# Attention of a hybrid diffusion step: exponentials scaled by the inverse denominators ahead of the transposes

## The reference

```python
def softmax_with_sink(s, sink):
    sk = sink.astype(jnp.float32).reshape(N_KV_HEADS, Q_PER_KV, 1, 1)
    m = jnp.maximum(jnp.max(s, axis=-1, keepdims=True), sk)
    e = jnp.exp(s - m)
    return e / (jnp.sum(e, axis=-1, keepdims=True) + jnp.exp(sk - m))
...
    p = softmax_with_sink(jnp.concatenate([s_lat, s_ctx], axis=-1), sink)
    o = (jnp.einsum('bnkgqs,bnskd->bnqkgd', p[..., :3 * BLOCK], vband)
         + jnp.einsum('bnkgqc,bckd->bnqkgd', p[..., 3 * BLOCK:], v_ctx.astype(jnp.float32)))
```

## Time and profile before

| what | us |
|---|---|
| median of three runs | 1802.57 (1801.4, 1802.57, 1913.08) |
| the profiled execution | 1803.81 |
| its span | 1802.0 |
| TensorE busy | 1722.3 (96%) |
| VectorE busy | 1034.3 (57%) |
| ScalarE busy | 808.0 (45%) |
| GpSimd busy | 386.9 (21%) |

### The profile page before, as it was taken

The page is one execution under the profiler, slowest core; times in us unless marked ns, Lnnn a source line. Parts: engine busy times, 40 slices in busy tenths (PEclk is TensorE's granted clock), DMA queues, the critical chain, the costliest instruction groups (busy, mean ns, idle before and its releaser), DMA issues.

```text
span 1802.0 us, 45799 instructions
## 1 busy us (share of the span) xinstructions
PE 1722.3 (96%) x19547; PEld 1621.0 (90%) x19547; DVE 1034.3 (57%) x2257; ACT 808.0 (45%) x1715; POOL 386.9 (21%) x318
## 2 busy tenths in 40 slices
PE   7999998899999999999999999898999999999997
PEld 5999776779899999999989987677799999999997
DVE  5445666663583673738453556675629648365663
ACT  4433655552453452525453356464335425344352
POOL 2344010223303002020434521002260110201113
PEclk9999999999999999999999999999999999999999
DMA  9755301004613223241346270010031231323211
GB/s 329 227 141 161 99 5 49 7 15 146 172 43 99 71 71 94 68 109 53 100 141 176 71 211 5 18 34 7 26 104 32 73 98 59 106 62 92 85 57 59
DMA packets 215972, 161.09 MB, mean 89 GB/s; under 512 B 21968, under 2 KB 213146, under 8 KB 215770
## 3 DMA queue, kind: packets, MB, share of 16 engines
q1 hardware_dynamic: 213818, 156.13, 29.7%
q0 software_dynamic: 1952, 2.03, 0.4%
HBM read 154.99 MB, written 3.15 MB: 88 GB/s over the span
## 4 chain that ended last, share of the span: by engine, by line
PE 85%; DVE 6%; ACT 4%; issue 3%; SPq 1%; DMA 1%; POOL 0%; ACTq 0%; DVEq 0%; POOLq 0%
PE PS L1143 27%; PE PS L1106 19%; PE PS L1107 19%; PE PS L1066 2%; PE PS L1400 2%; PE PS L1362 2%; PE PS L1385 1%; PE PS L1000 1%; DVE mix L2631 1%; DMA mix<-in_w_in 1%; ACT mix L2017 1%; SPq L776 1%; PE PS L1599 1%; PE PS L1643 1%; PE PS L984 1%
## 5 line engine op out<-in xcount | busy, mean ns | idle before, releaser
L2784 DVE SCALAR_TENSOR_TENSOR x<-PS,mod,x 128x320 f32<-128x320 f32 (+2 forms) x240 | 90.8, 434 | 283.8 <-PE PS L1107 283.8
L836 POOL TENSOR_TENSOR SfR<-ring,SfR 128x768 fp32r<-128x768 f32 (+1 forms) x24 | 41.1, 1714 | 627.6 <-ACT SfR L1862 627.6
L1143 PE MATMUL PS<-T_hi,wsplit 128*128 128x320 f32 x768 | 170.0, 309 | 0.0
L1106 PE MATMUL PS<-in_hi,win 128*128 128x320 f32 x480 | 150.0, 320 | 0.0
L1107 PE MATMUL PS<-in_hi,win 128*128 128x320 f32 x480 | 144.6, 309 | 0.0
L1106 PE MATMUL PS<-hid_hi,wsplit 128*128 128x320 f32 x440 | 132.9, 310 | 0.0
L1107 PE MATMUL PS<-hid_hi,wsplit 128*128 128x320 f32 x440 | 132.5, 309 | 0.0
L1143 PEld LDWEIGHTS PS<-T_hi,wsplit 128*128 128x128 f32 x768 | 128.4, 188 | 0.0
L1143 PE MATMUL PS<-h_hi,wsplit 128*128 128x320 f32 x576 | 127.6, 309 | 0.0
L1143 PE MATMUL PS<-T_lo,wsplit 128*128 128x320 f32 x384 | 118.7, 309 | 0.0
L2183 ACT ACTIVATE wsplit<-Sf 128x512 fp32r<-128x512 f32 x96 | 59.8, 628 | 127.8 <-DVE Sf L2834 70.1
(11 more groups left out here) (555 smaller groups left out, 5375.5 us busy)
## 6 DMA issues: line engine op xcount, KB each, us to landing
ring<-in_w_ada SPq DMA_DIRECT2D x47, 1024.0 KB, 7.6
ring<-in_ffn_w_in SPq DMA_DIRECT2D x88, 512.0 KB, 5.2
ring<-in_ffn_w_out SPq DMA_DIRECT2D x16, 768.0 KB, 4.4
ring<-in_ffn_w_out SPq DMA_DIRECT2D x16, 640.0 KB, 4.1
ring<-in_w_in SPq DMA_DIRECT2D x7, 1024.0 KB, 8.7
ring<-in_w_in SPq DMA_DIRECT2D x10, 512.0 KB, 5.8
ring<-in_w_in SPq DMA_DIRECT2D x16, 256.0 KB, 5.7
ring<-in_w_out SPq DMA_DIRECT2D x16, 256.0 KB, 6.0
```

The costliest lines, as they stand in the source:

```text
L836: nc.gpsimd.tensor_tensor(lo, raw_w, hi, SUB).then_inc(wl_ready(), 1)
L1106: mm(lat[:, 0:TH], w, v[:, 0:TH], start=(n == 0), stop=(n == total - 1))
L1143: last = mm(bank[:, 0:TH], (w_lo if p == 1 else w_hi)[:, k, :], (v_lo if p == 2 else v_hi)[:, k, :], start=(q in (A11, A12, S1_) and k == ...
L2784: last = V.scalar_tensor_tensor(x[:, m, a:b], bank[:, at:at + b - a], mod[:, gate_at + m, s:s + 1], x[:, m, a:b], MUL, ADD)
```

## The change

The four steps from the reciprocal on are reordered. `weights_scaled(m)` takes the reciprocal, waits for it, and multiplies the exponentials of both heads in place with the reciprocal of their row, a scalar per partition, with one `tensor_scalar` per head. The transposes then wait for `p_scaled`. The spreading products and the buffer for their copy are gone, and `normalise` is one copy from PSUM. On VectorE `weights_scaled(m-1)` comes first in the loop, ahead of `softmax_in(m)`. On TensorE `values(m-2)` comes ahead of `transposes(m-1)`.

```diff
@@ TensorE
                         for g in range(2):
                             n = 2 * m + g
-                            e.wait_ge(p_exp.sem, p_exp.upto(l, n + 1))
+                            e.wait_ge(p_scaled.sem, p_scaled.upto(l, n + 1))
...
-                                mm(bank[64 * g:64 * g + 64, 0:128], v, PT[:, m % 4, c, g, :],
-                                   start=(c == 0), stop=(c == len(tiles) - 1))
-                        e.wait_ge(den_inv.sem, den_inv.upto(l, m + 1))
-                        for g in range(2):
-                            last = mm(bank[64 * g:64 * g + 64, 128:256],
-                                      den[:, b % 2, j, g:g + 1].to_broadcast([128, 64]), ident, start=True, stop=True)
+                                last = mm(bank[64 * g:64 * g + 64, 0:128], v, PT[:, m % 4, c, g, :],
+                                          start=(c == 0), stop=(c == len(tiles) - 1))
                         last.then_inc(pv_done(), 1)
...
+                        if first <= m - 2 < last_pair:
+                            values(m - 2)
                         if first <= m - 1 < last_pair:
                             transposes(m - 1)
-                        if first <= m - 2 < last_pair:
-                            values(m - 2)
@@ VectorE
-                    def inverse(m):
+                    def weights_scaled(m):
                         b, j = ATT[m]
+                        w = 128 * len(key_tiles(b))
                         e.wait_ge(p_exp.sem, p_exp.upto(l, 2 * m + 2))
-                        V.reciprocal(den[:, b % 2, j, :], den[:, b % 2, j, :]).then_inc(den_inv(), 1)
+                        own.after(V.reciprocal(den[:, b % 2, j, :], den[:, b % 2, j, :]))
+                        for g in range(2):
+                            V.tensor_scalar(Pm[:, m % 3, g, 1:w + 1], Pm[:, m % 3, g, 1:w + 1],
+                                            den[:, b % 2, j, g:g + 1], None, MUL).then_inc(p_scaled(), 1)
...
-                        own.after(V.tensor_copy(inv_row[:, m % 2, :], bank[:, 128:256]))
-                        V.tensor_tensor(qt[:, j, 128 * b:128 * b + 128], bank[:, 0:128], inv_row[:, m % 2, :], MUL).then_inc(o_sb(), 1)
+                        V.tensor_copy(qt[:, j, 128 * b:128 * b + 128], bank[:, 0:128]).then_inc(o_sb(), 1)
 
                     for m in range(first, last_pair + 3):
+                        if first <= m - 1 < last_pair:
+                            weights_scaled(m - 1)
                         if m < last_pair:
                             softmax_in(m)
                         if first <= m - 3 < last_pair:
                             normalise(m - 3)
-                        if first <= m - 1 < last_pair:
-                            inverse(m - 1)
```

More of the change, by code:

```diff
@@ L471, in build @@
         PT = mix[:, PB + 6 * RAW_W:PB + 6 * RAW_W + 4096].rearrange("p (m c g t) -> p m c g t", m=4, c=4, g=2)
-        inv_row = mixv(PB + 6 * RAW_W + 4608, 256).rearrange("p (m t) -> p m t", m=2)
         stout = ush[0:64, 7, 0:512].rearrange("p (h a t) -> p h a t", h=2, a=2)
@@ L555, in build @@
         p_exp = sig("p_exp", 2 * NATT)
-        den_inv = sig("den_inv", NATT)
+        p_scaled = sig("p_scaled", 2 * NATT)
         pt_ps, pt_sb = sig("pt_ps", 2 * NATT), sig("pt_sb", 2 * NATT)
```

## The result

Median 1818.03 us over four runs (1817.09 to 1819.38), beside 1803.67 for the kernel before on the same chip: ratio 1.0083, 95% interval 1.007 to 1.0097. One of the four runs before, 1913.08, was in a slower state and is left out of the ratio. That is slower by 12.6 to 17.5 us: less than the 2% of the verdict, but more than the forecast of +10.5. The profiled executions say the same: 1818.85 against 1803.81, +15.04.

The account below looks back on a forecast made before the run. TensorE bounds the kernel before; after the change a dependence ring through VectorE's scaling does. 2 layers x (2.72 pass A + 2.51 pass B) = +10.5 us on the median of 1802.57 gives 1813, stated as 1814; range 1805 to 1824.

Parts of the forecast that it names:

- The ring: VectorE: softmax_in, exponentials, scaling, next softmax_in in sequence, nothing overlapped; 3.45, 2.96, 2.01 us with four, three, one tiles.
- price per scaling: VectorE: one tensor_scalar takes 0.48, 0.415 or 0.28 us for 512, 384 or 128 elements.
- overlap of 0.08: VectorE: an operation that waits for nothing starts about 0.08 us before the one ahead ends.
- step 11: Pass B, VectorE: preparation in two halves, some 1.85 us, outlasts the exponentials and adds 0.81 to an interval.
- step 12: Pass B, VectorE: preparation of 1.47 us, outlasts the exponentials and adds 0.67 to a three-tile interval.
- Tail of pass A: From the last softmax_in's start to the first product matmul: 6.40 us before, 6.00 after, 0.40 less.
- Pass B: Twelve pairs: last softmax_in starts 2.91 us later, tail shrinks from 3.69 to about 3.29; +2.51 us per layer.
- Recurrence: Follows each pass in the same dependence and shifts whole.
- TensorE as the bound (1): TensorE still sets the pace and 0.25 us per pair is saved: 1794 us; chance 0.08.
- Single rate (2): VectorE scalings last as long as L2845 (685 ns at 512 elements): 10 us more, 1824; chance 0.08.
- Another engine in the way (3): Another engine's memory access stretches a VectorE scaling by up to 2 us; 36 us when 13 of 80 hit; chance 0.03.
- The second ring (4): Copy, values, transposes, scores, exponentials also bind: 0.1 to 0.2 us more per four-tile pair, 1816 to 1822; chance 0.06.

Follow-up runs that it names:

- Experiment 2: Changed kernel with each scaling preceded by a second one, by ones, each waited for; ratio 1.0273, median 1855.24 us.
- experiment 7: Changed kernel with scaling behind softmax_in on VectorE and transposes, copies, values and normalise one pair later, values still ahead of transposes; ratio 1.0057.
- experiment 9: Changed kernel with scaling behind softmax_in, everything behind it one pair later, and transposes ahead of values on TensorE; ratio 0.9993.
- experiment 1: Changed kernel with TensorE's old order, transposes(m-1) ahead of values(m-2); ratio 1.0052.
- experiment 10: The changed kernel run and profiled a second time, nothing altered, beside the filler version; ratio 1.0085, median 1819.49 us.
- experiment 6: Changed kernel with VectorE's old order, weights_scaled(m-1) behind softmax_in(m) and normalise(m-3); ratio 1.0241, median 1844.11 us.
- experiment 3: Kernel before without the spreading products and the multiplication by them, attention left unnormalised; ratio 0.9962.
- experiment 5: Kernel before with only TensorE's new order, values(m-2) ahead of transposes(m-1), spreading kept and no scaling; ratio 1.0057.
- filler: Changed kernel plus 14 and 6 unread identity transposes early in pass A: ratio 1.0065, rerun 1.0075; with TensorE's old order too, 1.0052.

## Why the prediction was right, and where its sizes were off

**The ring was right.** The forecast gave 3.45, 2.96 and 2.01 between one X and the next for four, three and one tile; measured 3.41 (3.48 where a bonus step stands in between), 2.93 and 1.98 to 2.03 (2.21 for the first interval with one tile). Its price per scaling, 0.48, 0.415 and 0.28, came out at 485, 417 and 284 ns. Taking L2921 for the longer length, less L2336's slope, was good to 5 ns. The overlap of 0.08 holds too: the scalings begin at 225.95, and two operations of 0.485 would end at 226.92, but the next one starts at 226.74. The interval with step 11 was 4.28 (forecast 4.26), that with step 12 3.81 (3.63; the step started at X + 1.55, not X + 1.37). Experiment 2 shows that the ring is the bound, by lengthening it. Experiments 7 and 9 show the same from the other side: with every scaling kept and a pair more in between, the ring is gone.

**The size, from +10.5 to +15.04.** The ring without the new order on TensorE, experiment 1, measures 1.0052, which is +9.4 (6.3 to 12.5), and its passes A are 2.8 longer than before, where the forecast had 2.72. So the term of the scaling in pass A was right, though two small misses cancel in it (ring 0.14 shorter, tail 0.24 longer), and other terms made up the rest. That the miss is not larger owes something to luck, as the recurrence below shows.

- *Tail of pass A: +1.53 per layer over the forecast* (7.53, forecast 6.00). This is the step that failed. The forecast let the last transposes follow the last scaling, and so left out `values(6)`, which the order puts ahead of them and which waits for a copy behind the last exponentials. In its paragraph on the order it had said that the order helps, since the values would use TensorE's idle time. The intervals of experiment 1 show that there was nothing to help: but for the one of 4.63, those of pass A are equal with either order. Experiment 1 puts 1.29 of the 1.53 down to the order; its own tail, 6.24, leaves 0.24 that I did not take apart. I had worked out the wait that the old order puts before the values, and not the one that the new order puts before the transposes.
- *Low clock at X2 to X3: +1.70 per layer*, in both profiles of the changed kernel. It was not in the sum. The gaps that the forecast named ("TensorE idle before transposes") are what stands ahead of it, 2.00 us before 205.75. That such gaps are enough is not shown. Experiment 1 has gaps as long or longer in the same place, and its windows stay at 1.00 there:

```profile
205.44 0.64 PEld L1384 LDWEIGHTS PS<-mats,mix 128*128 128x128 f32 x6 [1.99 <-DVE mix L2562]
...
208.37 0.64 PEld L1384 LDWEIGHTS PS<-mats,mix 128*128 128x128 f32 x6 [1.39 <-DVE mix L2562]
```

The Trainium skill, "TensorE: Matmul & The Clock Gate", Part 1, says that full speed is what activity releases, and that the same kernel shows different numbers of slow matmuls at its start from run to run. The traces agree with the first, and here slow stretches in the middle differ from run to run too: 0.50 behind the idle stretch, and low stretches at the entry of pass B in one profile of the changed kernel and not in the other (39.41 and 38.24 for the same pass).
- *Pass B: +3.08 and +4.71* against 2.51. Three of these four passes have a low stretch at their entry, the exception being layer 1 before. It costs 1.62 before (36.33 against 34.71) and 1.17 after (39.41 against 38.24 in experiment 10). The pair without one is 34.71 and 38.24: +3.53. Of the 1.0 over the forecast, 0.3 is the tail (3.62, forecast 3.29), 0.2 the intervals behind X9 (step 12 above all), and 0.5 the interval from X8 to X9. The forecast let X9 stay where the modulation matmuls set it. But its 4.06 us before are the length with the low stretch: without one the interval takes 2.96 before (layer 1) and 3.42 after, which is the ring.
- *Recurrence: -4.0*. The forecast shifted it whole. It got shorter in both layers. What differs in the traces are a few long waits of TensorE, put down to "issue", inside runs of small matmuls. The waits of TensorE's loads in layer 1's recurrence (total us, times, longest), before and then after:

```profile
PEld PS L1572 <- issue: 1.9, 1, 1.9
...
PEld PS L1589 <- issue: 1.2, 1, 1.2
```

```profile
PEld PS L1577 <- issue: 1.6, 1, 1.6
PEld PS L1538 <- issue: 1.2, 2, 0.8
```

They are no scatter of a single run. The wait at L1577 stands at the same statement in both profiles of the changed kernel and in experiments 1, 2, 6, 7 and 9 (1.05 to 1.60 us), and in experiment 3, where this statement is L1578. All of these have TensorE's list without the spreading (19387 loads). The kernel before and experiment 5, with 19547, share the waits at L1572 and L1589, and the three profiles with filler have theirs at other lines. So the places go with the length of TensorE's list. The recurrence between the passes goes with it too: in both layers together it takes 108.5 and 108.7 us in the two kernels with spreading and 102.8 to 106.4 in the eleven profiles without. Experiment 3, which scales nothing, has 103.5. So the credit seems to come with dropping the spreading and not with the scaling; what makes the waits stays open. Without this credit the sum would have been off by 8.5 us and not by 4.5: two misses of opposite sign, and that they offset each other was luck.

So 10.5 + 2 x 1.53 + 2 x 1.70 - 0.2 (the ring of pass A slightly shorter) + 2.8 (both passes B) - 4.0 - 0.5 = 15.1, with 15.0 measured.

**The rivals.** TensorE as the bound (1): false, within a pass softmax_in waits for scores only where the clock is low (1.61 in pass A) and once for 0.16; and its price was too high, since without spreading the kernel gains 6.9 us by the ratio (0.0038 x 1806.64), 5.6 by the passes, and not 10. Single rate (2): false, 485 ns against 685. Another engine in the way (3): no scaling was stretched; the means are those above. The second ring (4): false for the changed kernel, whose intervals in pass A don't depend on the order but for the clock. True for the kernel before with the new order (experiment 5), and its place was the right one to look at: the order does cost, once a pass and not once a pair. The measured 1818 lies in that rival's range, but not by its mechanism.

**The signs.** The forecast looked for idle time of TensorE before transposes, some 0.3 per pair. It stands before the values instead (columns as in the earlier trace rows), because these come first and wait for ScalarE's copy, whose row is the first (it ends at 223.26, and the values start at 223.38):

```profile
222.20 1.06 ACT L2023 ACTIVATE mix<-PS 128x512 f32<-128x512 f32 x2
...
223.38 0.67 PEld L1399 LDWEIGHTS PS<-mix 128*64 128x64 f32 x12 [0.89 <-issue]
...
224.44 0.85 PEld L1384 LDWEIGHTS PS<-mats,mix 128*128 128x128 f32 x8 [0.17 <-issue]
...
226.79 0.66 PEld L1399 LDWEIGHTS PS<-mix 128*64 128x64 f32 x12 [0.39 <-issue]
```

The forecast's last sign was about the shift: products late by 2.7 and 2.5 us, and the end with them. The passes are in fact 5.8 and 5.9 us longer (A) and 3.1 and 4.7 (B), and the end came 15.0 later and not 19.5, since the recurrence did not shift whole.

## What to carry to other kernels

In a loop whose engines run in written orders, moving work from the busy engine to an idle one pays only if it doesn't close a ring: follow the moved step to its input and to the next instruction behind it on its engine, and add up the way round. Busy shares (95% and 58% here) say nothing of that. Work out an order for the middle of the loop, the first steps and the last one each; the ends are where this one cost. A ring is opened by putting a whole iteration between the producer and the consumer (experiment 9), but each iteration more is paid again in the tail.

## What the runs showed of the hardware that I had not expected

- Half clock behind a short idle stretch in the middle of dense work: 0.50 over 208 to 212, cost 1.70 us, after TensorE's loads had been idle for 2.00 us. Experiment 1 had 1.99 us of idle time at the same place and kept the full clock, so the idle time alone does not decide it. The filler removed it there; low stretches stand elsewhere with and without filler. Runs of experiment 1 go from 1809.59 at a mean granted clock of 0.996 to 1819.47 at 0.988: the runs of one kernel spread with the clock over 9.9 us, nearly this change's forecast.
- A tensor_scalar with one pointer follows one line over the sizes: 284, 417 and 485 ns for 128, 384 and 512 elements, 0.52 to 0.53 ns per element.
